# Products with the streams' states: the states become the moving operand, in four column groups of the array

## The reference

```python
def gated_delta_chunked(q, k, v, g, beta, s0):
    ...
    def step(s, inp):
        q_i, k_i, u_i, w_i, qk_i, g_i = inp
        v_new = u_i - jnp.einsum('bhcd,bhde->bhce', w_i, s)
        o_i = (jnp.einsum('bhcd,bhde->bhce', q_i * jnp.exp(g_i)[..., None], s)
               + jnp.einsum('bhij,bhje->bhie', qk_i, v_new))
        g_last = g_i[..., -1:]
        s = (s * jnp.exp(g_last)[..., None]
             + jnp.einsum('bhcd,bhce->bhde', k_i * jnp.exp(g_last - g_i)[..., None], v_new))
        return s, o_i
    s_final, o = lax.scan(step, s0, (qc, kc, u, w, qk, gc))
```

## Time and profile before

| what | value |
|---|---|
| median of 3 runs | 1291.66 us (1290.34 to 1295.38) |
| profiled execution, its own time | 1291.4 us |
| its span, first to last instruction | 1289.2 us |
| PE busy | 1245.0 us (97%) |
| DVE, ACT, POOL busy | 594.8, 411.6, 132.6 us |
| granted clock of PE, mean | 0.982 of full speed |
| chain that ended last, PE's share | 92% |

### The profile page before, as it was taken

One profiled execution on the slowest core, in us unless ns is written; L12 is line 12 of the kernel. 1 busy time (PEld: TensorE's weight loads), 2 busy tenths in 40 slices (PEclk: granted clock), 3 DMA queues, 4 the chain that ended last, 5 costly groups with the idle time before them and its releaser, 6 DMA issues.

```text
span 1289.2 us, 19036 instructions
## 1 busy us (share of the span) xinstructions
PE 1245.0 (97%) x7705; PEld 1093.1 (85%) x7705; DVE 594.8 (46%) x815; ACT 411.6 (32%) x754; POOL 132.6 (10%) x90
## 2 busy tenths in 40 slices
PE   8998998999999799998999999999999999999997
PEld 8996566788776588887999998899998998898876
DVE  2664855423355756554333334534332442333347
ACT  3444311221223466664222222233321231132120
POOL 3330003013004321121000000200000000000000
PEclk9998999999988899999999999999999999999999
DMA  6225201000521613322221234012322222222222
GB/s 225 68 81 54 49 33 34 18 1 1 184 57 46 233 42 107 107 90 99 74 77 70 73 92 137 1 51 80 108 83 71 75 72 82 66 82 82 82 82 82
DMA packets 54380, 101.54 MB, mean 79 GB/s; under 512 B 12208, under 2 KB 33200, under 8 KB 53680
## 3 DMA queue, kind: packets, MB, share of 16 engines
q1 hardware_dynamic: 54320, 100.68, 25.3%
HBM read 94.21 MB, written 7.38 MB: 79 GB/s over the span
## 4 chain that ended last, share of the span: by engine, by line
PE 92%; DVE 4%; ACT 2%; DMA 1%; issue 1%; POOL 0%; SPq 0%; DVEq 0%
PE psum L591 44%; PE psum L1029 21%; PE psum L672 6%; PE psum L691 6%; PE psum L651 2%; PE psum L673 2%; PE psum L697 1%; PE psum L933 1%; PE psum L861 1%; PE psum L715 1%; PE psum L951 1%; PE psum L1038 1%; PE psum L849 1%; PE psum L912 1%; PE psum L897 1%
## 5 line engine op out<-in xcount | busy, mean ns | idle before, releaser
L591 PE MATMUL psum<-x_high,w_high 128*128 128x320 f32 x768 | 178.5, 310 | 4.9 <-DVE w_low L1412 4.9
L591 PE MATMUL psum<-x_low,w_high 128*128 128x320 f32 x768 | 178.2, 310 | 0.0
L591 PE MATMUL psum<-x_high,w_low 128*128 128x320 f32 x768 | 177.9, 310 | 0.0
L1412 DVE TENSOR_TENSOR w_low<-raw,w_high 128x1024 fp32r<-128x1024 f32 (+1 forms) x80 | 107.7, 1346 | 134.7 <-ACT w_high L1832 133.5
L1832 ACT CAST w_high<-raw 128x1024 fp32r<-128x1024 f32 (+1 forms) x80 | 90.8, 1135 | 165.2 <-PE psum L1029 155.4
L591 PEld LDWEIGHTS psum<-x_high,w_high 128*128 128x128 f32 x768 | 129.5, 189 | 5.7 <-issue 3.9
L591 PEld LDWEIGHTS psum<-x_low,w_high 128*128 128x128 f32 x768 | 129.7, 189 | 0.0
L591 PEld LDWEIGHTS psum<-x_high,w_low 128*128 128x128 f32 x768 | 129.6, 189 | 0.0
L1029 PE MATMUL psum<-w_high,hid_high 128*128 128x512 f32 x280 | 109.7, 392 | 0.0
L1029 PE MATMUL psum<-w_high,hid_low 128*128 128x512 f32 x280 | 109.7, 392 | 0.0
L1029 PE MATMUL psum<-w_low,hid_high 128*128 128x512 f32 x280 | 109.6, 392 | 0.0
(11 more groups left out here) (310 smaller groups left out, 2314.4 us busy)
## 6 DMA issues: line engine op xcount, KB each, us to landing
raw<-w_tiles SPq DMA_DIRECT2D x72, 512.0 KB, 3.5
raw<-w_mix SPq DMA_DIRECT2D x16, 768.0 KB, 4.3
ring<-w_h SPq DMA_DIRECT2D x12, 512.0 KB, 3.5
ring<-w_piece SPq DMA_DIRECT2D x24, 256.0 KB, 2.8
work<-w_h SPq DMA_DIRECT2D x9, 512.0 KB, 3.5
work<-cmkT SPq DMA_DIRECT2D x8, 512.0 KB, 3.7
work<-cmv SPq DMA_DIRECT2D x8, 512.0 KB, 4.6
mem_w<-w_mem SPq DMA_DIRECT2D x11, 256.0 KB, 2.7
```

The lines of the kernel that those rows point to most:

```text
L591: mm = pe.matmul(ps[b0 + half][:, 0:HALF], weights[weight][:, c], act[part][:, k, half * HALF:(half + 1) * HALF], start=start and k == 0 a ...
L1412: dve.tensor_tensor(w_low[slot][:, 0:width], raw[slot][:, 0:width], w_high[slot][:, 0:width], ALU.subtract).then_inc(sem("low_out"), 1)
```

## The change

The operands of the two products change places. The streams' tokens become the stationary operand: those of two neighbouring streams stand in 32 columns, and four such pairs fill the four column groups of the array, each writing 32 partitions (tokens) of PSUM. The states' 128 value columns are the moving operand. As the two streams of a pair have different states, each pair takes two matmuls that add up: in the first the columns of the second stream are zero, in the second those of the first. POOL makes these spaced operands (`spaced`): for keys and queries one memset of the zeros and one copy for each head. The result has tokens on the partitions. So the keys' product is written straight into the bank of `ks` of tile 4, and the four transposes there go. The queries' product takes the place of `kst` in the order, is copied by ACT as before, and enters `go` of tile 4 by four matmuls with the identity. Two semaphores become one (`kv_mm`), a third is new (`spaced_out`).

```diff
+        spaced = [arena[:, Q0 + 9 * TOK + 768 * i:Q0 + 9 * TOK + 768 * (i + 1)].rearrange("p (h g x) -> p h g x", h=H, g=4)
+                  for i in range(2)]
...
+            def stream_states(stage, n, rows):
+
+                pe.wait_ge(sem("s0_in"), 48)
+                pe.wait_ge(sem("spaced_out"), 2)
+                b = heads(bank(stage, n)[:, :])
+                for h in range(H):
+                    for e in range(2):
+                        for g in range(4):
+                            mm = pe.matmul(b[32 * g:32 * g + 32, h, :], rows[:, h, g, ST * e:ST * e + 32],
+                                           S0[:, h, 2 * g + e, :], start=e == 0, stop=e == 1,
+                                           tile_position=(0, 32 * g))
+                mm.then_inc(sem(f"{stage}_mm"), 1)
...
                 if stage == "ks" and t == 4:
-                    pe.wait_ge(sem("kst_out"), 1)
-                    per_head_transpose("ks", n, lambda h: kst_sb[:, h, :])
+                    stream_states("ks", n, spaced[0])
...
+                    if t == 4:
+                        pe.wait_ge(sem("kst_out"), 1)
                     for h in range(H):
...
-                        pe.matmul(b[:, h, :], vn_streams[:, h, :], QKD[:, 4, h, :], start=True, stop=False,
-                                  skip_group_check=True)
-                        for j in range(NB):
-                            c = slice(NP + j * ST, NP + (j + 1) * ST)
-                            mm = pe.matmul(b[:, h, j * ST:(j + 1) * ST], S0[:, h, j, :], qkv3[:, h, c],
-                                           start=False, stop=j == NB - 1, skip_group_check=True)
+                        pe.matmul(b[:, h, :], kst_sb[:, h, :], ident, start=True, stop=False)
+                        mm = pe.matmul(b[:, h, :], vn_streams[:, h, :], QKD[:, 4, h, :], start=False, stop=True)
...
                 if stage == "kst":
-                    pe.wait_ge(sem("s0_in"), 48)
-                    b = heads(bank("kst", 0)[:, :])
-                    for h in range(H):
-                        for j in range(NB):
-                            c = slice(NP + j * ST, NP + (j + 1) * ST)
-                            mm = pe.matmul(b[:, h, j * ST:(j + 1) * ST], S0[:, h, j, :], qkv3[:, 4 + h, c],
-                                           start=True, stop=True)
-                    mm.then_inc(sem("kst_mm"), 1)
+                    stream_states("kst", 0, spaced[1])
...
+            pool.wait_ge(sem("xt_mm"), level_count("xt", 6, TT - 2) + 1)
+            pool.wait_ge(sem("qe_out"), TT)
+            for i, first in enumerate((4, 0)):
+                pool.memset(spaced[i][:, :, :, ST:2 * ST], 0.0)
+                for h in range(H):
+                    x = spaced[i][:, h].rearrange("p g (e x) -> p g e x", e=3)[:, :, 0::2, :]
+                    last = pool.tensor_copy(x, qkv3[:, first + h, NP:TOK].rearrange("p (g e x) -> p g e x", g=4, e=2))
+                last.then_inc(sem("spaced_out"), 1)
```

More of the change, by code:

```diff
@@ L808, in chunk_product @@
                         mm = pe.transpose(ps[6 + x // 4][:, (x % 4) * P:(x % 4 + 1) * P], h3[:, W_V, tok(x)], ident)
-                    mm.then_inc(sem("vtok_mm"), 1)
+                    mm.then_inc(sem("kv_mm"), 1)
                     return
@@ L816, in chunk_product @@
                             mm = pe.transpose(b, mkv[:, st, h * P:(h + 1) * P], ident)
-                    mm.then_inc(sem("mkT_mm"), 1)
+                    mm.then_inc(sem("kv_mm"), 1)
                     return
@@ L1356, in chunk_step @@
                 if stage == "vtok":
-                    dve.wait_ge(sem("vtok_mm"), 1)
+                    dve.wait_ge(sem("kv_mm"), 1)
                     dve.tensor_copy(arena[:, P0 + 2048:P0 + 2560], ps[6][:, :]).then_inc(sem("kv_out"), 1)
@@ L1360, in chunk_step @@
                 if stage == "mkT":
-                    dve.wait_ge(sem("mkT_mm"), 1)
+                    dve.wait_ge(sem("kv_mm"), 2)
                     for j in range(2):
```

## The result

The changed kernel takes 1272.61 us, the median of 4 runs (1271.17 to 1273.35), against 1291.18 us of the kernel before beside it: a ratio of 0.9848, 95% interval 0.9825 to 0.9872. The forecast was 1273.5. The profiled execution took 1273.35 us, 18.05 less than that of before; the forecast for this difference was 18.1.

A forecast was written before the change was run, and what follows sets the result against it. PE, with 92% of the chain, was taken as the bound: 14.72 direct plus 4.99 clock, less 0.2, 0.15 and 1.3, gives 18.1 us off 1291.4, so 1273.3, forecast as 1273.5 for the median; range 1269.5 to 1281.5.

The forecast's parts named there:

- The two new stages: On PE, replacing `kst` and the `ks` transposes: 64 records each at 32 ns, 2.02 us a stage, 4.04 for two.
- the switch: PE entering and leaving the column-group form, judged by idle time before L968: cost 0.2 us, bounds 0 and 0.7.
- `go` of tile 4: On PE, eight 128 x 128 matmuls at 0.22 us replace the old product: 1.76 us instead of 10.03.
- The clock: Half-clock matmuls behind both products return to full clock, judged by L968's steady record lengths: 4.99 us back, bounds 0 and 4.99.
- direct saving: On PE, 20.52 us removed less 5.80 added: 14.72 us.
- The building: POOL's ten operations for `spaced`: 2.5 to 4.0 us, hidden before `kst`; DVE's wait at L1370 taken as 0.15 us.
- POOL's scaling: After g, the release by `go` of tile 4, DVE meets the scaling and `x_low`: 1.3 us lost before `ks` of tile 3.
- The sum: Whole execution: 19.71 - 0.2 - 0.15 - 1.3 = 18.1 us off, passing whole to the end.
- The groups that take turns: Rival in the two new stages: 0.11 us a record, 7.0 us instead of 2.02 a stage, 1283.5 us; chance 0.04.
- The clock that falls all the same: Rival on PE around the products: each fall costs 5.5 us; one gives 1279, two 1284.5; chance 0.08.
- the memory steps that wait for loads: Rival in the memory steps: no change, as loads landing in 13 us would eat the whole saving; chance 0.04.
- the POOL that holds up `kst`: Rival ahead of `kst`: PE waits for `spaced_out`; slower, 1298 us and more, from 37.6 us of building; chance 0.03.

The follow-up runs named there:

- Experiments 1 and 3: Kernel before, only the keys' product in the new form: 1281.69 us; kernel before, all 128 stream tokens moved per state instead of 16: 1282.95 us.
- experiment 6: Changed kernel with POOL's building of the spaced operands held back until `ks` of tile 1, so nothing covers it: 1276.04 us, 0.9889 of the kernel before.
- experiment 4: Changed kernel with POOL's eight scalings of `S0` released by `ks` instead of `go` of tile 4, ahead of the second `x_low`: 1272.28 us.
- the changed kernel's second profile: From the changed kernel run again unaltered, as yardstick on another chip: 1272.54 us, 0.9866 of the kernel before.
- experiments 1 to 5: Experiments 1 and 3, experiment 2, experiment 4, and a fifth: experiment 4's kernel with the scan's first and last `x_low` waiting for DVE's `ds`: 1270.92 us.
- eight comparisons: The changed kernel, its repeat and the six experiment kernels, each against the kernel before on the same chip: ratios 0.9845 to 0.9940.
- experiment 2: Changed kernel with all 64 matmuls of the two products in the first column group, streams' outputs not computed: 1282.68 us.

## Why the prediction was right, step by step

- **The two new stages.** Forecast 4.04 us, and 0.2 for entering and leaving. Measured 1.88 and 1.89. The matmul behind each takes 0.20 and 0.19 more than it does elsewhere (L879 1.06 against 0.86, L654 1.91 against 1.72), so 4.16 against 4.24. The sum is that near because two errors cancel: the stages were put 0.27 too high, and the switch, which the prediction bounded by the idle time ahead of L968, 0.19 too low. That the cost of the switch lies behind the stage fits the drain that the Trainium skill ("TensorEngine Tiling (Array Packing)", section "Key Properties") describes, at 0.2 us; no run took it away, so that cause is not shown.
- **`go` of tile 4.** Forecast 1.76, measured 1.78.
- **The clock.** All 4.99 us behind the products came back, forecast so. Experiments 1 and 3 tie each fall to its own product with 16 moving columns. What the prediction didn't set apart is that the 14.72 us of its direct saving held as much of the clock again: at full clock `kst` is 7.15 us with even 128 moving columns, not 10.05, and `go` some 2 us shorter.
- **The building.** Hidden, as forecast: POOL's last copy ended at 337.65 us, ten microseconds ahead of `kst`. L1376, which stood for 0.15 us, took 0.69 as before; POOL waited instead, and its second four copies took 1.47 us, not 1.00 (the rows below). That each microsecond beyond the cover would be paid in full was too little: in experiment 6 a wait of 3.14 us also cost 1.7 us of clock.

```profile
334.72 0.31 POOL L2049 MEMSET arena<- 128x256 f32 x1 [14.62 <-PE psum L694]
334.98 1.00 POOL L2052 COPY arena<-arena 128x128 f32<-128x128 f32 x4
335.92 0.31 POOL L2049 MEMSET arena<- 128x256 f32 x1
336.18 1.47 POOL L2052 COPY arena<-arena 128x128 f32<-128x128 f32 x4
```

- **POOL's scaling.** The mechanism was right and the size too large: 1.3 us forecast, 0.9 measured. With g = 373.38, L1379 ended at g + 11.97, where g + 12.35 was forecast; in experiment 4 it ended at 385.72, which is 11.04 from its own g of 374.68 (the start of the memory step behind `go`); the prediction gave g + 11.05 without the meetings.
- **The sum.** The scan became 18.76 us shorter: 20.52 - 5.55 for the stages, less 0.39 behind them, plus 4.99, less 0.9, and 0.1 of smaller gaps. Of the profiled execution's span, 18.0 us are gone. The prediction let the saving pass whole to the end, and in this execution it didn't: between `ks` of tile 3 and the first product with `o_high` 38.32 us passed instead of 37.11, while `vn` of tile 0 had begun 0.88 us earlier, ahead of all that was changed. That 18.05 came out where 18.1 was forecast is therefore partly luck: the scan saved 0.66 us more, and what lies around it took back 0.7. In the changed kernel's second profile the stretch behind the scan takes 37.18 us. The difference is the clock behind a wait for a load; first the profile after, then the second:

```profile
420.00:422.00 2.00, 2.00 (x10) 2.00 (x9) 1.02 (x3) 2.00 (x9) 0.81 (x1) 0.54 0.64 199
```

```profile
420.00:422.00 2.00, 2.00 (x16) 2.00 (x15) 1.02 (x3) 1.98 (x8) 1.41 (x1) 1.00 0.88 306
```

  Whether this fall belongs to the change stays open. The 24 records of L594 (L591 before) behind that wait take 5.29 to 5.31 us in the first profile after and in those of experiments 1 to 5, and 3.8 us in the kernel before, in the second profile after and in experiment 6. And in all eight comparisons the median gains 0.2 to 2.3 us less than the scan (18.57 against 18.76 here, 17.15 against 18.77 in the second). Each of these gaps lies within the interval of its ratio, and the eight share one profile of the kernel before, so they don't show that the tail takes back part of the saving; that all have one sign speaks for it.

- **The rivals.** The groups that take turns are what experiment 2 made, at 1282.7 us where 1283.5 was worked out. The clock that falls all the same, the memory steps that wait for loads and the POOL that holds up `kst` were not seen in the changed kernel's scan.

## What to carry to other kernels

A product with few moving columns can lose twice, as this one did: a record of 16 columns took nearly as long as one of 128, and the clock fell in it and behind it, so that the stages behind paid too; read the granted clock of the stretch after it. Where such products are many, exchange the operands and put the narrow one in column groups, but see that neighbours in the order use different groups: in experiment 2 the narrow load by itself saved nothing. And when a stage gets shorter, ask which work of the engines off the path it releases sooner, and whose operations that work now meets.

## What the hardware showed that was not expected

A matmul's record doesn't tell whether groups work side by side. In one group and in four, L813 has the same durations; only the spacing differs, 0.111 us against 0.029. Here is the line in the kernel with one group (ns, min/median/max), and then in the changed one:

```profile
L813 PE MATMUL psum<-work,arena x128: 272/273/297, 348.3 to 367.7; 128*32 128x128 f32 x128
```

```profile
L813 PE MATMUL psum<-work,arena x128: 272/273/297, 347.7 to 356.6; 128*32 128x128 f32 x128
```

The prediction took L968's unchanged record lengths as a sign of the clock. That sign wasn't empty: in experiment 6, where the clock fell, L813's longest record was 421 ns instead of 297. But the granted clock of the stretch says it directly.
